# Moving one convolution and one set of exponentials in the SSD groups of a three-layer block

## The reference, cut to what matters

```python
z, xbc, dt_raw = split(hn @ w_in)
xbc = silu(depthwise_conv_centered(xbc, conv_w, conv_b))     # 5 taps, along the positions
xs, bm, cm = split(xbc)
dt = softplus(dt_raw + dt_bias);  log_a = dt * A
y = bidir_scan(cm, bm, xh * dt[fwd], xh * dt[bwd], log_a[fwd], log_a[bwd])   # chunks of 128
y = (y + xh * d_skip) * silu(z)
y = y * rsqrt(mean(y * y, per group) + eps) * norm_g
return y @ w_out
```

## Time and profile before

| | us |
|---|---|
| median of 3 executions | 1065.94 |
| the three | 1063.35, 1065.94, 1067.65 |
| the profiled execution, its own time | 1063.7 |
| its span | 1061.9 |
| group 0 of the SSD stage on PE | 396.0 to 441.1 |
| group 1 | 441.1 to 486.7 |
| group 2 | 486.7 to 534.3 |

### The profile page before, as it was taken

The page is one execution under the profiler, slowest core; times in us unless marked ns, Lnnn a source line. Parts: engine busy times, 40 slices in busy tenths (PEclk is TensorE's granted clock), DMA queues, the critical chain, the costliest instruction groups (busy, mean ns, idle before and its releaser), DMA issues. The chain is left out here.

```text
span 1061.9 us, 16225 instructions
## 1 busy us (share of the span) xinstructions
PE 1001.1 (94%) x6261; PEld 882.7 (83%) x6261; DVE 484.2 (46%) x980; ACT 619.6 (58%) x1127; POOL 692.1 (65%) x548
## 2 busy tenths in 40 slices
PE   5999989999999799999899799999998998999988
PEld 4898769999998798788778699999986887877867
DVE  3745344434434466575644544444253143223553
ACT  6636565554555676486756655545555478855631
POOL 3977526765776488576647566665767755865654
PEclk9999998999999899999999899999998999999999
DMA  9774415765555375644525456556555645634220
GB/s 327 239 205 153 148 51 182 250 228 195 192 167 151 104 230 163 190 148 139 199 97 166 142 183 207 165 192 197 181 178 164 163 159 178 210 128 159 83 77 40
DMA packets 131946, 178.69 MB, mean 168 GB/s; under 512 B 21457, under 2 KB 94045, under 8 KB 131677
## 3 DMA queue, kind: packets, MB, share of 16 engines
q1 hardware_dynamic: 127693, 169.95, 49.6%
q10 hardware_dynamic: 4176, 7.71, 2.2%
HBM read 176.51 MB, written 5.24 MB: 171 GB/s over the span
## 5 line engine op out<-in xcount | busy, mean ns | idle before, releaser
L505 POOL TENSOR_TENSOR wlo<-raw,whi 128x512 fp32r<-128x512 f32 x512 | 670.2, 1344 | 344.3 <-ACT whi L1109 344.1
L520 PE MATMUL PS<-Th,whi 128*128 128x256 f32 (+1 forms) x1008 | 291.1, 289 | 4.1 <-DVE Tl L1595 3.0
L521 PE MATMUL PS<-Tl,whi 128*128 128x256 f32 (+1 forms) x1008 | 287.8, 285 | 0.0
L522 PE MATMUL PS<-Th,wlo 128*128 128x256 f32 (+1 forms) x1008 | 287.6, 285 | 0.0
L1109 ACT ACTIVATE whi<-raw 128x1024 fp32r<-128x1024 f32 (+1 forms) x150 | 157.1, 1047 | 179.0 <-PE PS L522 129.6
L517 PE MATMUL PS<-whi,Th 128*128 128x512 f32 (+1 forms) x512 | 206.7, 404 | 6.7 <-DVE Tl L1595 4.8
L1650 DVE SCALAR_TENSOR_TENSOR arena<-PS,cols,arena 128x255 f32<-128x255 f32 (+1 forms) x272 | 118.7, 478 | 189.8 <-ACT arena L1208 166.8
L520 PEld LDWEIGHTS PS<-Th,whi 128*128 128x128 f32 (+1 forms) x1008 | 194.6, 193 | 10.8 <-issue 6.3
L519 PE MATMUL PS<-whi,Tl 128*128 128x512 f32 (+1 forms) x512 | 200.3, 391 | 0.0
L518 PE MATMUL PS<-wlo,Th 128*128 128x512 f32 (+1 forms) x512 | 199.9, 390 | 0.0
L521 PEld LDWEIGHTS PS<-Tl,whi 128*128 128x128 f32 (+1 forms) x1008 | 194.8, 193 | 1.6 <-issue 0.7
(11 more groups left out here) (223 smaller groups left out, 1074.0 us busy)
## 6 DMA issues: line engine op xcount, KB each, us to landing
raw<-in_ffn_w_up_dram SPq DMA_DIRECT2D x44, 1024.0 KB, 5.1
raw<-in_ffn_w_down_dram SPq DMA_DIRECT2D x22, 1024.0 KB, 4.9
raw<-in_w_in_dram SPq DMA_DIRECT2D x22, 1024.0 KB, 5.0
raw<-in_c_w_in_dram SPq DMA_DIRECT2D x16, 1024.0 KB, 6.2
raw<-in_ab_w_in_dram SPq DMA_DIRECT2D x14, 1024.0 KB, 6.3
raw<-in_c_w_out_dram SPq DMA_DIRECT2D x8, 1024.0 KB, 6.5
raw<-in_ab_w_out_dram SPq DMA_DIRECT2D x4, 1024.0 KB, 5.0
raw<-in_c_w_in_dram SPq DMA_DIRECT2D x8, 512.0 KB, 5.3
```

The source lines that it names most:

```text
L505: i = nc.gpsimd.tensor_tensor(wlo[n % NLO][:, c:e], raw[n % NRAW][:, c:e], whi[n % NHI][:, c:e].bitcast(F32), ALU.subtract)
L520: mm(o, wh, ah, start=first, stop=False)
L521: mm(o, wh, al, start=False, stop=False)
L522: return mm(o, wl, ah, start=False, stop=last)
```

## The change

On ACT, the exponentials of block 3 stand ahead of `ssd_centre(g + 1, 1)`, with the rounding in it, and not behind. On DVE, the skip additions and masked blocks 4 and 5 stand ahead of the second x convolution of the next group, `ssd_conv(g + 1, 1)`, and not behind. PE's, POOL's and SP's programs are as before. For g = 3 nothing changes.

```diff
                 high(b + 4)
                 exps(2)
+                exps(3)
                 if more:
                     ssd_centre(g + 1, 1)
-                exps(3)
                 exps(4)
                 exps(5)
                 high(b + 5)
...
                 masked(2)
                 masked(3)
-                if more:
-                    ssd_conv(g + 1, 1)
                 dve.wait_ge(*at("s_yie", g))
                 for c in range(NT):
                     i = tt(y[:, c, :], y[:, c, :], xs[g % 2][:, c, :], ALU.add)
                 lk(i)
                 masked(4)
                 masked(5)
+                if more:
+                    ssd_conv(g + 1, 1)
                 ssd_tile(g, 0)
                 masked(6)
                 masked(7)
```

## The result

The changed kernel took 1051.29 us in the median of 4 executions (1050.62 to 1051.84), the kernel before 1064.81 us (4 executions). The ratio is 0.9863, with a 95% interval of 0.984 to 0.9885. Two later measurements of the same kernel gave ratios of 0.9881 (0.9862 to 0.9901, median 1054.32) and 0.9883 (0.9857 to 0.991, median 1052.9).

A forecast was written before the change was run, and what follows sets the result against it. TensorE bounds the kernel (busy 1001.1 of 1061.9 us), losing time to waits and low clock. Savings of 11.1 us less 1.7 us for one low stretch give 9.4 us: 1065.9 - 9.4 = 1056.5 us, range 1053 to 1062.

The forecast's parts named there:

- What bounds, and what is late next: Groups 0 to 2: PE's 6.8 us of masked-product waits bound; block 6 is late next, new waits 0, 0.4, 0.4 us.
- The sum: Savings in groups 0, 1 and 2 of 4.3, 2.4 and 4.4 us, together 11.1 us without new low stretches.
- I take one ... 1.7 us. Gain 9.4 us.: Groups 0 to 2: one stretch at 1.2 GHz comes back, costing 1.7 us of the 11.1 us.
- the bounds (none and three): Low-clock stretches that come back in groups 0 to 2: none or three, costing 0 or 5.1 us.
- The small bounds: Possible losses behind group 0 (up to 0.5 us) and at the tile's multiplication (up to 1.1 us per group), costed at 0.
- The silu of group 0: Gap behind group 0: silu ends near 435.4, PE's transposes ask at 435.8; cost 0, at most 0.5 us.
- the tile ahead of block 6: DVE's multiplication at L1888, groups 0 to 2: POOL could stretch it by up to 1.1 us each; taken as 0.
- The wait did not move: Rival, groups 0 to 2: waits move to block 6, gain only 2.2 us, about 1063.7; moved or lost gain 0.15.
- Earlier transfers: Rival, SP's queue: earlier weight transfer delays block 5's sums, up to 8 us slower, 1074; chance 0.05.
- a sign of being wrong: Sign at POOL in the groups: waiting longer than 1.9 us for the sums of block 5.
- the gain is swallowed in the layer behind: Rival, layer behind the stage: transfers limit it, so 1066 us; counted as no change, moved or lost gain 0.15.

The follow-up runs named there:

- the tile moved: Changed kernel with the first output tile behind masked block 7 in groups 0 to 2; medians 1050.62 and 1049.81 us, ratios to before 0.9858 and 0.988.
- DVE's part alone: Kernel before with only the skip additions and masked blocks 4 and 5 ahead of the second convolution; 1064.36 us, ratio to before 0.9986.
- the one with the skip additions early: DVE's part alone, with the skip additions also moved ahead of masked block 3; 1053.5 us, ratio 0.9886 to the kernel before.

## Why the prediction was wrong, by its own steps

*What bounds, and what is late next: right.* PE's waits ahead of pairs (2,3) and (4,5) went, and block 6 became the late one, with 0, 0.47 and 0.48 us for the 0, 0.4 and 0.4 worked out.

*The sum: right in all, by groups within 0.3 us.* 4.3, 2.4 and 4.4 us, together 11.1, were measured as 4.58, 2.23 and 4.27, together 11.08. A pair that PE does not wait for takes 1.70 us in the changed kernel (465.09 - 463.39), not the 1.81 that I had read.

*The step that failed: "I take one ... 1.7 us. Gain 9.4 us."* The number of low stretches that come back in the three groups was the one term of the sum without a row, and it was none: none in four profiles of the change, and none in two with the tile moved, with waits of 0.48 us at most. I had the bounds (none and three), wrote that the waits were shorter than any that a low stretch had followed, and still took a stretch off. Without it the forecast would have been 1065.9 - 11.1 = 1054.8 us, inside half a percent of all three measurements.

*The rest of the difference.* 11.1 us is not yet 13.5. The mean over four profiles each is 124.4 against 112.9 us for the groups, 11.6 us, since one of before had 125.8. Outside the groups the means are 939.7 and 937.7 us, but with spreads of 6.1 and 4.1 us, so those 2.0 us can't be told from chance. The first measurement of the change also lay low (1051.3, then 1054.3 and 1052.9). I had taken the gain off one median and drawn the range with 3.5 us on the fast side, which did not hold both a wrong term of 1.7 us and this scatter. Whether the end of the stage helps the parts behind it stays open.

*The small bounds.* The silu of group 0 ended at 433.56 and PE's transposes began at 434.42, without waiting: 0.9 us in hand where I had 0.4. POOL did collide with DVE, but on the skip additions (2.69 us in group 1, hidden) and not on the tile ahead of block 6 (L1888 at 0.69 us in all three groups). I had written of these additions only that DVE was idle there. That they are hidden hangs on the other half of the change, which the prediction treated as worth 1.07 us in two groups: with DVE's part alone nearly the whole gain is lost, with either the exponentials or the additions earlier it is there.

*The rivals.* The wait did not move in the whole change; it did in each half of it. Earlier transfers did not hold up the sums in group 1: POOL waited 1.32 us for those of block 5, not 1.90. In group 2 it waited 2.71 us (2.30 before), more than the 1.9 us that I had named as a sign of being wrong, but the exponentials of block 5 still followed those of block 4 without a gap, so nothing was held up. That the gain is swallowed in the layer behind did not happen.

## What to carry to other kernels

When a chain on one engine feeds another at several points, sum the chain up to each point in the new order, and check where an instruction with slack behind it would stand without that slack: here two moves were each worth next to nothing and together about 12 us, because each only moved the wait. A term that no row shows is better taken at the value that the rows around it favour, and the range, not the forecast, carries the other values. And before a few microseconds are explained, profile both kernels more than once: in the changed kernel the part that the change touches repeated to 0.04 us, the untouched rest did not repeat to 4 us.

## What the runs showed of the hardware

The clock fell behind waits in a way that I had not expected to be so sharp. In the three groups, over all fourteen profiles, PE waited 1.92 us or longer for a masked product 14 times, and the granted clock went to 1.2 GHz right behind, or in, all 14 of them, for 3.4 us or 6.8 us. It waited 1.71 to 1.76 us three times and never lost clock. Of twelve waits of 0.93 to 1.02 us two were followed by a low stretch, and of the single waits of 0.61 and 0.78 us and eight of 0.44 to 0.48 us none. It is no fixed rule: in group 3, ahead of pair (0,1), PE waited 1.92 to 2.01 us for another line of DVE in all fourteen profiles, and in three of them full clock followed, in the first profile of before after 1.99 us. A long wait removed can be worth more than itself: from DVE's part alone to the one with the skip additions early, 2.1 us of waiting in each of two groups went, and the groups shortened by 5.4 and 4.3 us.
